# A hybrid encoder block on one core: the front of each delta-rule head made at the end of the head ahead of it

## What is computed

```python
a_qkv = jax.nn.silu(causal_conv(a_qkv, conv_w))      # 4 taps, for q, k and v of each head
beta = jax.nn.sigmoid(a_beta)
g = -jnp.exp(a_log) * jax.nn.softplus(a_dec + dt_bias)
# gated_delta_rule, per head: q, k normalised, gc = cumsum(g) in a chunk
decay = jnp.exp(jnp.where(tril, gc[..., :, None] - gc[..., None, :], -jnp.inf))
L = jnp.where(strict, einsum('nbhik,nbhjk->nbhij', kb, kc) * decay, 0.0)   # kb = k * beta
sol = triangular_solve(L + eye, concatenate([vb, kb * exp(gc)]))           # vb = v * beta
attn = einsum('nbhik,nbhjk->nbhij', qc, kc) * decay
def step(state, inp):                                # chunk after chunk
    v_new = uu - ww @ state
    o = qd @ state + at @ v_new
    state = state * cd + kd.T @ v_new
# behind the rule, per head:
o_a = o_a * rsqrt(mean(o_a * o_a) + eps) * gdn_norm_w * silu(z)
```

## Time and profile before

| | us |
|---|---|
| median of 3 runs | 2066.95 (2064.85 to 2073.45) |
| the profiled execution | 2069.85 |
| its span, first to last instruction | 2068.2 |
| PE busy in the span | 1874.3 (91%) |
| DVE busy | 1047.8 (51%) |
| ACT busy | 652.5 (32%) |
| POOL busy | 354.3 (17%) |

### The profile page before, as it was taken

How to read it: one execution, slowest core, us unless ns; L and a number is a source line. 1 busy time by engine, 2 the same in 40 slices (tenths; PEclk the granted TensorE clock), 3 DMA queues, 4 the chain that set the end, 5 groups by cost and what they waited for, 6 DMA issues and landing times.

```text
span 2068.2 us, 25709 instructions
## 1 busy us (share of the span) xinstructions
PE 1874.3 (91%) x10544; PEld 1140.5 (55%) x10544; DVE 1047.8 (51%) x1750; ACT 652.5 (32%) x1061; POOL 354.3 (17%) x290
## 2 busy tenths in 40 slices
PE   5999999999999998999799999899899898898993
PEld 4877777777777776888634333333334333333431
DVE  6546645654652446423745545445455454443546
ACT  5423322332332556112323331322322313223133
POOL 0423322332332321445000000000000000000000
PEclk9999999999999998999799999999999999999996
DMA  8322212222222211545789999999999999999992
GB/s 264 82 60 59 60 47 62 62 62 62 62 69 54 70 62 41 223 134 176 289 356 402 405 403 408 407 398 412 403 407 415 396 402 406 393 411 399 413 416 114
DMA packets 170997, 504.94 MB, mean 244 GB/s; under 512 B 18400, under 2 KB 108640, under 8 KB 117504
## 3 DMA queue, kind: packets, MB, share of 16 engines
q1 hardware_dynamic: 167696, 490.56, 62.4%
q0 software_dynamic: 2608, 8.53, 1.5%
q10 hardware_dynamic: 576, 4.19, 0.5%
HBM read 498.92 MB, written 12.71 MB: 247 GB/s over the span
## 4 chain that ended last, share of the span: by engine, by line
PE 47%; DMA 34%; DVE 12%; ACT 3%; issue 3%; SPq 1%; DVEq 0%; ACTq 0%
DMA ring<-in_w_up 34%; PE bank L1749 9%; PE bank L2138 8%; PE bank L1751 8%; PE bank L1750 8%; PE bank L2147 2%; PE bank L2107 2%; PE bank L1884 1%; DVE gd_L L1332 1%; PE bank L1875 1%; PE bank L1893 1%; DVE att L1389 1%; DVE sc L1384 1%; DVE half L1193 1%; DVE sc L1404 1%
## 5 line engine op out<-in xcount | busy, mean ns | idle before, releaser
L2138 PE MATMUL bank<-ring,xbT 128*64 128x512 f32 x2048 | 489.7, 622 | 78.7 <-DMA ring<-in_w_up 76.3
L1623 DVE TENSOR_TENSOR r<-r,bank 128x512 f32<-128x512 f32 x496 | 307.3, 681 | 233.7 <-PE bank L2107 233.7
L635 POOL TENSOR_TENSOR wlo<-raw,whi 128x512 fp32r<-128x512 f32 x232 | 313.3, 1382 | 591.2 <-ACT whi L748 459.4
L2138 PEld LDWEIGHTS bank<-ring,xbT 128*64 128x64 f32 x2048 | 156.6, 142 | 365.0 <-issue 362.6
L1749 PE MATMUL bank<-hTh,wlo 128*128 128x512 f32 x704 | 304.9, 433 | 0.7 <-DVE hTl L1126 0.6
L1751 PE MATMUL bank<-hTh,whi 128*128 128x512 f32 x704 | 279.6, 397 | 0.0
L1750 PE MATMUL bank<-hTl,whi 128*128 128x512 f32 x704 | 279.5, 397 | 0.0
L2147 PE MATMUL bank<-ring,hidT 128*64 128x512 f32 x992 | 219.7, 595 | 0.5 <-ACT hidT L1032 0.5
L1628 DVE TENSOR_TENSOR yhl<-yw,yhl 64x512 fp32r<-64x512 f32 x128 | 88.2, 689 | 219.1 <-ACT yhl L1043 216.1
L683 POOL DMA_INDIRECT xb<-h_scr,idx_tok x32 | 29.8, 931 | 890.2 <-PE bank L2114 876.5
L748 ACT ACTIVATE whi<-raw 128x2048 fp32r<-128x2048 f32 x50 | 95.6, 1913 | 227.7 <-PE bank L1751 227.7
(11 more groups left out here) (346 smaller groups left out, 2047.7 us busy)
## 6 DMA issues: line engine op xcount, KB each, us to landing
ring<-in_w_gate SPq DMA_DIRECT2D x128, 1024.0 KB, 28.7
ring<-in_w_up SPq DMA_DIRECT2D x128, 1024.0 KB, 29.0
ring<-in_w_down SPq DMA_DIRECT2D x128, 1024.0 KB, 28.4
raw<-in_w_in SPq DMA_DIRECT2D x44, 1024.0 KB, 5.6
raw<-in_w_o SPq DMA_DIRECT2D x16, 1024.0 KB, 5.1
xt<-in_x SPq DMA_DIRECT2D x4, 1024.0 KB, 9.1
h_scr<-xt SPq DMA_DIRECT2D x4, 1024.0 KB, 7.9
r<-h_scr SPq DMA_DIRECT2D x1, 4096.0 KB, 12.2
```

What stands on the lines that cost most here:

```text
L635: i = pool.tensor_tensor(wlo[sl][:, part, :], raw[sl][:, :].rearrange("p (k n) -> p k n", k=KD)[:, part, :], whi[sl][:, part, :].bitcast(F ...
L1623: dve.tensor_tensor(v, v, comb_bank(q, tt)[:, :], ALU.add).then_inc(comb_done, 1)
L2138: i = mm(GU[SLOTS * h:SLOTS * (h + 1), :], xT_[:, k, :], w[:, kk * F:(kk + 1) * F], start=k == 0, stop=k == KD - 1)
```

## The change

Each iteration no longer begins with the front of its own head. The front of head `it + 1` is made at the end of iteration `it`, while head `it` still has its last sums to do: the transposes of k, the decay row, the grams (`keys`, `queries` on PE), squares and decay exponentials (`ahead` on ACT), differences, norms, L, A and x64 (`decay_steps`, `norms`, `gdn1` on DVE). What is left of head `it`, the reciprocal, norm and gate (`finish`), moves behind it to the start of iteration `it + 1`. For the first head the front stands ahead of the loop. The 64 k-steps are shared out anew: 12, 14, 24 in the levels, 11 in the scan, 1, and 2. With this move:

- the v transposes go to bank BS instead of B0, the A transposes to B1 instead of BM, and `gb` lies where x64 and xt64 lie;
- the parameter copy `hp` and the per-head tap copy `cwh` are gone: DVE reads `tokpar` and `cw` directly (the taps are halved once, ahead of the loop);
- the root of the key norms is taken of the sum and inverted on DVE (a reciprocal of 128x4 more), and both roots of an iteration stand side by side on ACT;
- the convolution of v is split: its first two steps in the scan, the other two behind the decay differences; ACT copies out the v strip after the scan's first chunk instead of its last;
- `vb`, xt64 and the squares of q stand in `values`, at the start of the head's own iteration;
- POOL's mask stands ahead of the iteration's first `lo`.

The diff, cut to its core (the same edits of `hp` and `cwh` into `par(n, i)` and `w_a` are left out):

```diff
-        gb = at("gb", ATT + 2 * KB * names.index("A"), [P, TT, P])
+        gb = at("gb", ATT + 2 * KB * names.index("X"), [P, TT, P])
...
+                if gdn:
+                    pool.wait_ge(dec_exp, it)
+                    ed = T["Ed"][:, :].rearrange("p (c i) -> p c i", c=TT)
+                    pool.affine_select(out=ed, in_=ed, compare_op=ALU.is_ge, fill=0.0, base=0,
+                                       pattern=[[0, TT], [-1, P]], channel_multiplier=1).then_inc(dec, 1)
...
+            def key_root(n):
+                act.wait_ge(kss_done, n)
+                act.activation(kn[:, K_V, :], kn[:, K_SS, :], ACT.Sqrt, bias=eps[:, 1:2]).then_inc(kn_root, 1)
+
+            def out_root(n):
+                act.wait_ge(o_ss, n)
+                act.wait_ge(dec_exp, min(n + 1, HEADS))
+                act.activation(T["dm"][:, :], BM[:, :], ACT.Sqrt, bias=eps[:, 2:3], scale=1.0 / DK).then_inc(o_root, 1)
...
                 next_hi(it, 0)
-                if gdn:
-                    out_z(it - 1)
-                    gdn0(it)
+                out_z(it - 1)
+                gdn1(it)
                 next_hi(it, 1)
                 out_k(0) if last else out_qkv(it, 0)
-                if gdn:
...
+                    if c == 0 and not last:
+                        out_qkv(it, 2)
                     if c < 2:
                         hi_half(4 * it + 5, slot(4), loads(it, 4), c)
-                    elif c == TT - 1:
-                        out_v(0) if last else out_qkv(it, 2)
+                    elif c == TT - 1 and last:
...
                 gdn3(it, between)
                 if not last:
+                    ahead(it + 1)
                     tanh(it, 2)
+                    key_root(it + 1)
+                out_root(it)
...
+            ahead(1)
+            key_root(1)
...
-            def gdn0(n):
-                h = n - 1
-                act_silu(0, n)
-                act_silu(1, n)
-                dve.tensor_copy(hp[:, :, :].rearrange("p f c -> p (f c)"),
-                                tokpar[:, bass.ds(h, 1), :, :].rearrange("p o f c -> p (o f c)")).then_inc(hp_ready, 1)
-                dve.wait_ge(hp_ready, n)
-                dve.tensor_copy(gb[:, :, :], over(hp[:, 2, :])).then_inc(gb_ready, 1)
-                act_silu(2, n)
-                act_silu(3, n)
+            def decay_columns(n):
+                dve.tensor_copy(gb[:, :, :], over(par(n, 2))).then_inc(gb_ready, 1)
+
+            def decay_steps(n):
...
+            def values(n):
...
+            def output_squares(n):
...
+            def finish(n):
...
-                if not last:
-                    conv_weights(it)
                 if gdn:
-                    gdn0(it)
-                    gdn1(it)
+                    act_silu(2, it)
+                    if it > 1:
+                        finish(it - 1)
+                    act_silu(3, it)
+                    values(it)
...
+                if not last:
+                    decay_columns(it + 1)
+
+                def between(c):
+                    if c < TT - 1 and not last:
+                        conv(it, 2, [c - 1])
+
...
-                    scan(it)
+                    scan(it, between)
                 if not last:
-                    conv(it, 2)
+                    act_silu(1, it + 1)
                 if gdn:
-                    finish(it)
+                    output_squares(it)
+                if not last:
+                    W(dve, o_sum, it)
+                    act_silu(0, it + 1)
+                    decay_steps(it + 1)
+                    conv(it, 2, range(2 if gdn else 0, CONV))
+                    norms(it + 1)
+                    gdn1(it + 1)
...
-
-                feed(11)
+            def keys(n):
...
+            def queries(n):
+
+                pe.wait_ge(silu[0], n)
                 for c in range(TT):
...
-                feed(9)
...
+            def gdn(n, feed):
+
+                feed(12)
...
                 i.then_inc(tr_ps, 1)
+                pe.wait_ge(silu[2], n)
+                pe.wait_ge(kss_done, n)
+                pe.wait_ge(vk_done, nth(n, 2, 0))
...
-                feed(4)
-
-                pe.wait_ge(tr_done, nth(n, 2, 0))
+                feed(14)
+
+                pe.wait_ge(tr_done, 2 * n)
                 pe.wait_ge(x_init, 4 * n)
-                pe.wait_ge(vk_done, 2 * n)
...
+                pe.wait_ge(vk_done, 2 * n)
...
-                feed(3)
-                pe.wait_ge(o_sum, n)
-                mm(BM[:, :], ones, T["A"][:, :], start=True, stop=True).then_inc(o_ss, 1)
+                if n < HEADS:
+                    keys(n + 1)
+                feed(1 if n < HEADS else 3)
+                output_norm(n)
+                if n < HEADS:
+                    queries(n + 1)
...
+            pe.wait_ge(par_done, 2)
+            keys(1)
+            queries(1)
             for it in range(1, HEADS):
                 feed = steps(it)
-                pe.wait_ge(par_done, 2)
```

More of the change, by code:

```diff
@@ L480, in build, with par @@
         K_SS, K_INV, K_L, K_R, K_V = range(5)
-        KN = 5
+        KN = 6
+        def par(n, i):
+            return tokpar[:, n - 1, i, :]
         def diag(name, h):
@@ L777, in out_z @@
                 act.wait_ge(strip_mm, 4 * it + 5)
+                W(act, silu[3], it)
                 act.activation(half[3][:, :], PA[0][:, :], ACT.Copy, scale=0.5)
@@ L784, in tanh, with ahead @@
                 act.activation(th[j][:, :], half[j][:, :], ACT.Tanh).then_inc(tanh_done, 1)
-            def gdn0(n):
+            def ahead(n):
                 act.wait_ge(tr_ps, nth(n, 4, 0))
@@ L790, in gdn0 @@
                 for c in range(TT):
-                    i = act.activation(T["X"][:, c * P:(c + 1) * P], BS[:, c * P:(c + 1) * P], ACT.Square,
+                    i = act.activation(T["LT"][:, c * P:(c + 1) * P], BS[:, c * P:(c + 1) * P], ACT.Square,
                                        accum_out=kn[:, K_SS, c:c + 1])
@@ L803, in gdn1 @@
                 act.wait_ge(tr_ps, nth(n, 4, 2))
-                act.activation(T["attnT"][:, :], BM[:, :], ACT.Copy).then_inc(tr_done, 1)
+                act.activation(T["attnT"][:, :], B1[:, :], ACT.Copy).then_inc(tr_done, 1)
             def gdn3(n, between):
@@ L1278, in gdn1 @@
                 dve.wait_ge(kn_root, n)
-                dve.tensor_tensor(kn[:, K_V, :], kn[:, K_V, :], hp[:, 1, :], ALU.mult).then_inc(kn_step, 1)
+                dve.reciprocal(kn[:, K_V, :], kn[:, K_V, :]).then_inc(kn_step, 1)
+                dve.wait_ge(kn_step, nth(n, KN, 4))
+                dve.tensor_tensor(kn[:, K_V, :], kn[:, K_V, :], par(n, 1), ALU.mult).then_inc(kn_step, 1)
                 dve.wait_ge(kn_step, KN * n)
                 dve.wait_ge(tr_ps, 4 * n)
-                dve.tensor_tensor(tiles("vb"), psum_tiles(B0), over(kn[:, K_V, :]), ALU.mult).then_inc(vk_done, 1)
+                dve.tensor_tensor(tiles("vb"), psum_tiles(BS), over(kn[:, K_V, :]), ALU.mult).then_inc(vk_done, 1)
                 dve.wait_ge(qd_done, n)
@@ L1308, in level, with scan @@
                     dve.tensor_scalar(tiles("XT")[HALVES[0], :, HALVES[1]], ps64(B2, HALVES[0]), -1.0, None, ALU.mult).then_inc(xtu, 1)
-            def scan(n):
+            def scan(n, between):
                 for c in range(TT):
@@ L1315, in scan @@
                                                  in1=tiles("vb")[:, c, :], op0=ALU.mult, op1=ALU.add).then_inc(rr_done, 1)
+                        between(c)
                     if c < TT - 1:
@@ L1369, in _ @@
             iteration(HEADS, last=True)
+            finish(HEADS)
             def group(m):
@@ L1837, in gdn @@
                 i.then_inc(gc_row, 1)
-                pe.wait_ge(silu[0], n)
                 for c in range(TT):
@@ L1844, in gdn, with output_norm @@
                 i.then_inc(gram_qk, 1)
-                feed(9)
+            def output_norm(n):
+                pe.wait_ge(o_sum, n)
+                W(pe, o_root, n - 1)
+                mm(BM[:, :], ones, T["A"][:, :], start=True, stop=True).then_inc(o_ss, 1)
+            def gdn(n, feed):
+                feed(12)
                 pe.wait_ge(exp_row, n)
```

63 lines of the change are left out of this document (21 added, 42 removed).

## The result

The changed kernel took 2019.62 us (median of 4 runs, 2017.50 to 2021.24), the kernel before 2067.93 us beside it (4 runs, 2064.85 to 2073.45): ratio 0.9763, 95% interval 0.9740 to 0.9786. On a second chip the same pair gave 0.9762 (0.9739 to 0.9785). The profiled execution took 2019.17 us with a span of 2017.5 us, 50.7 us less than the 2068.2 us before.

What follows compares the result with a forecast made beforehand. PE, busy 91% of the span, was taken as the bound. Ending its loop waits and slow clock gives 53.5 us, less 6 for the first head and 0.7 for switches: 46.8 saved, 2020 us from 2066.95, range 2010 to 2042.

Steps and rivals of the forecast that it cites:

- The four waits: PE's waits in the head loop for `vb`, silu of k, `gb` and output squares; with drains and slow clock, 53.5 us.
- list of signs: What would show the forecast: four waits gone, first level 4.9 us at clock 1.00, head period from 71.8 to about 65.2.
- The silu of k: On DVE after the scan's last `rr`: 1.77 us beside POOL, needed about 2.2 us after, hidden by 0.4 us.
- The squares: Output squares, behind only the silu of k: PE reaches their sum some 1.7 us after `o_sum`, wait 0, 5.6 us removed.
- A: On DVE, all there 8.2 to 8.9 us after `o_sum`; PE reaches L's transposes at 13.1 us, margin over 4 us.
- The k strip's split: Next k strip, tightest deadline: ready 14.4 us after `o_sum`, needed at PE's seventeenth k-step at 17.0, margin 2.6 us.
- B: Rival: moved two-input DVE steps collide with POOL, some waits return, 21 us less gained, 2041 us; chance 0.20.
- C: Rival: the k strip's rounding or split comes late, PE waits for `wlo`; 2091 us at 10 us delay; chance 0.07.
- D: Rival: nothing arrives at the end, through the experts' weights or an unseen wait; 2060 to 2070 us; chance 0.07.
- The first head: Cost of the change: PE idles 2.3 us for k, then slow clock and a late k strip; 6 us, bounds 3 and 9.
- `vb`: 17.4 us of idle time and 14.4 us of slow clock: Ahead of the levels: 8 waits of PE for `vb` with drains, plus the slow first level behind them over eight heads.
- The excess over 4.87 us: First level's extra time behind the `vb` wait, taken as slow clock: 3.43 us in head 1, 1.48 in head 8.

Runs made afterwards that it cites:

- refeed_sq: Kernel before with k-steps shared anew, nothing moved, but 3 instead of 4 ahead of the output squares' sum, so only that wait returns: 2020.61 us, ratio 0.9776.
- vb_only: Kernel before with 7 k-steps instead of 4 ahead of the levels, taken from second halves of the last three levels: 2061.11 us, ratio 0.9958.
- k_only: Kernel before with 15 k-steps instead of 11 ahead of the k transposes, taken from second halves of the last four levels: 2033.57 us, ratio 0.9841.
- one_wait: refeed with 1 k-step instead of 7 ahead of the levels and 10 instead of 4 in the first level's first half: 2039.74 us, ratio 0.9876.
- first_head: Changed kernel with the first head's front reordered: k's convolution and tanh first, its strip split sooner, q grams behind two k-steps: 2019.58 us, ratio 0.9784.
- vb_full: Kernel before with 7 k-steps instead of 4 ahead of the levels and 4 in the first level's first half, taken from the levels: 2041.92 us, ratio 0.9885.
- refeed: Kernel before with only its k-steps shared anew (15 ahead of the k transposes, 7 ahead of the levels), nothing moved between heads: 2016.69 us, ratio 0.9766.

## Why the prediction was right, and where its reasons were not

**The sum.** 46.8 us saved were forecast, 49.1 us were gained by the end of the loop in the traces, and 48.3 us by the medians. The four waits and their slow stretches went together, and nothing took their place: the forecast's case. Of the 2.3 us more in the traces, about 1.5 are a second slow stretch in head 2 that the forecast missed and 0.5 the cheaper first head.

**The steady head.** Forecast 65.2 us by its list of signs, measured 65.1. Of the 7.0 us a head that went from head 1 to head 8, the brackets of the earlier trace rows are 4.7 (18.5 / 7 and 2.0), four drains at 0.15 are 0.6, and 1.7 are left for the slow clock, against 1.5 to 1.8 in the forecast; 0.2 of these are head 2's second stretch. With the drain of 0.03 that refeed_sq shows, 0.5 us more would fall to the clock, so the split between the two is less sure than their sum. The first level lasts 5.09 us, not the 4.9 of the forecast's signs.

**The deadlines**, in us. The silu of k ran beside POOL, 1.79 where 1.77 was taken, ended at 283.24 and the transposes began at 283.74: hidden, as narrowly as said. The squares were summed 1.65 after `o_sum` (284.56 to 286.21), forecast 1.7, no wait. A was there at 291.5, L half a microsecond sooner, PE came at 297.54: a margin of 6 where over 4 was said. The k strip's split ended at 298.20 and PE took its first piece at 301.59: a margin of 3.4, forecast 2.6. POOL took 5.22 where the worst row of 6.44 was counted, and the rounding ended 0.3 us later than the forecast had it. On ACT the instruction behind the table load starts 0.01 us after its 1.28 us. The page of the Trainium skill ("ScalarE: Activation LUTs", What ACT_TABLE_LOAD costs) has 2.66 us for a switch; this trace doesn't show it, and the row was the one to take.

**Rivals.** B: two-input steps did meet POOL (the silu of k 1.79 us), which agrees with the rule cited from "SBUF — State Buffer" in the Trainium skill, but each within its margin. C: no wait for `wlo` after the first head. D: the end moved by more than the loop's end.

**The first head.** Forecast an idle 2.3 us, k at 88.4 and 6 us in all. Measured an idle 2.10 us, k transposes at 87.98, clock 0.77 in the 7 us behind it (1.6 us of that stretch), waits of 0.56 for v and 0.84 for `wlo`: with their drains some 5.5 us.

**What failed: the price of a single wait.** The step "`vb`: 17.4 us of idle time and 14.4 us of slow clock" describes the kernel before, but is wrong as a term. Covering `vb` alone gave 5 us (vb_only), covering it with `a` 23, covering k and `gb` alone 31, where the list had 31.8, 31.8 and 16.1. The sum came out since the change covered every wait at once; for half a change it would have been off by 9 to 27 us. In that the right number owes something to luck.

One reason is shown: things stand in a row on ACT and DVE. Covering k and `gb` made `vb` 1.67 us earlier, and behind `vb` stands `a`, which comes so late that the first level lasts 6.26 us even at full clock (k_only). The excess over 4.87 us that the forecast put down to the clock alone has two causes that hide each other.

The other reason is shown only in so far as the forecast's rule falls. "PE had idled for 2.0 us, and matmuls behind it ran for a while at the lower level" doesn't hold in general: behind 2.33 us it did so in half the heads (one_wait), behind 2.65 us in first_head it did not, and behind pieces of 1.0 us it did in every head of vb_only and in one of seven of vb_full, where the same pieces stand in the same places. What takes the rule's place stays open. The head's sum of idle time puts the table in rough order only.

**And the front's place** was never needed (refeed). It costs the change its first head and gives nothing back but 0.3 us a head. What is shown for the gain itself is that it comes from PE not having to wait, since two different ways of arranging that give it.

What stays open is what decides between heads with equal waits, as in one_wait, and what the two short runs of vb_only looked like. A rival that no run tests is that the moment at which a wait falls counts, beside its length. It would fit the steady heads of the kernel before and of vb_only, which last 71.8 and 71.7 us though the second idles 0.65 us less. Moving the front only for heads 2 to 8 wasn't tried either; with the first head's 5.5 us back its loop would end at about 617 us, an estimate, where refeed's ended at 618.9.

## What to carry to other kernels

Where an engine that is otherwise full waits in a few places, first try to share its filler work anew, so that more of it stands ahead of each late value: a few counts in this kernel brought the whole gain of a reordering over four engines, and 4.9 us more. Price waits together, or run the halves: what one wait costs depends on the others, through the queues behind it and through the clock, and such prices don't add. And before a slow stretch is priced by its length, look at what the engine would wait for if it were fast.

## What the runs showed of the hardware

- Granted clock behind idle time, in the table above: 2.27 us of idle time a head in three pieces brought no slow stretch, 2.3 to 2.7 us brought one in some heads and not in others with equal waits, 3.3 us and more in all of them. No run separates the amount from the moment at which it falls.
- A slow stretch costs 1.4 to 1.6 us where nothing hides it (first levels of one_wait, 9.6 against 11.0 to 11.2 us; period of the one slow head of vb_full, 70.2 against 68.6 us), and 0.2 us where PE would else have waited for `a` (k_only).
- A wait of PE costs its bracket and 0.03 to 0.15 us (refeed_sq).
- Beside POOL's subtractions of 128x512 even a small DVE step stretches: 1.38 instead of 0.43 us for the second `xt` step, 1.79 instead of 0.69 us for a silu.
